# Prompt sparse attention rewritten block by block, key groups paired, probabilities scaled before their transposes

## The reference

```python
# 8 query heads, 2 key/value heads (K), 4 query heads for each (G), head dim 64
s = einsum('btkgd,bckd->bkgtc', qcg, k_cmp) * scale           # 63 compressed keys
p_cmp = _masked_probs(s, cmp_end <= q_pos)
o_cmp = einsum('bkgtc,bckd->btkgd', p_cmp, v_cmp)
imp = einsum('bkgtc,cs->bkts', p_cmp, c2s)                    # importance of 16 blocks of 64 keys
score = where(visible, imp + where(forced, 1e4, 0), NEG)
top_val, top_idx = top_k(score, 8)                            # 8 blocks chosen for each query and key head
p_sel = _masked_probs(q_rot @ k_sel, chosen and key_pos <= q_pos)
p_win = _masked_probs(q_rot @ kw, 0 <= q_pos - kw_pos < 512)  # sliding window
o = o_cmp * g[..., 0:1] + o_sel * g[..., 1:2] + o_win * g[..., 2:3]
```

## Time and profile before

| quantity | value |
|---|---|
| median of 3 runs | 3833.59 us |
| the profiled execution: its own time | 3827.84 us |
| its span in the trace | 3826.0 us |
| PE busy, of the span | 3136.7 us, 82% |
| DVE, ACT, POOL busy | 1184.1, 737.9, 273.9 us |
| mean granted clock of PE | 0.904 of full speed |

### The profile page before, as it was taken

How to read it: one execution, slowest core, us unless ns; L and a number is a source line. 1 busy time by engine, 2 the same in 40 slices (tenths; PEclk the granted TensorE clock), 3 DMA queues, 4 the chain that set the end, 5 groups by cost and what they waited for, 6 DMA issues and landing times. The chain is left out here.

```text
span 3826.0 us, 40607 instructions
## 1 busy us (share of the span) xinstructions
PE 3136.7 (82%) x13898; PEld 2038.5 (53%) x13898; DVE 1184.1 (31%) x2468; ACT 737.9 (19%) x1251; POOL 273.9 (7%) x291
## 2 busy tenths in 40 slices
PE   7886877775678999784566799667979999996999
PEld 4554546665556677552343344543446666664665
DVE  2333655453345555301230112221123323230000
ACT  3332431111023343200120111111111222120000
POOL 1110002221010101000000000000000010000000
PEclk9898988887589999897788899889989999998999
DMA  3111010001210000274755211352221111112211
GB/s 116 56 56 50 27 32 12 11 11 41 69 25 25 25 13 13 74 227 133 221 154 206 89 66 55 121 176 91 88 60 33 40 37 33 33 33 46 80 53 38
DMA packets 286044, 265.13 MB, mean 69 GB/s; under 512 B 68002, under 2 KB 250148, under 8 KB 285412
## 3 DMA queue, kind: packets, MB, share of 16 engines
q1 hardware_dynamic: 247684, 224.82, 18.8%
q10 hardware_dynamic: 38240, 38.84, 3.3%
HBM read 219.75 MB, written 48.04 MB: 70 GB/s over the span
## 5 line engine op out<-in xcount | busy, mean ns | idle before, releaser
L3030 PE MATMUL up_acc<-hnT,up_w 128*128 128x364 f32 (+1 forms) x2112 | 646.9, 470 | 11.6 <-DMA up_w<-in_w_up 11.6
L3030 PEld LDWEIGHTS up_acc<-hnT,up_w 128*128 128x128 f32 x2112 | 402.7, 191 | 255.5 <-issue 14.6
L3131 PE MATMUL down_acc<-mlp_gT,down_w 128*128 128x364 f32 (+1 forms) x1056 | 324.6, 471 | 29.9 <-DMA down_res<-scr_h2T 29.9
L3131 PEld LDWEIGHTS down_acc<-mlp_gT,down_w 128*128 128x128 f32 x1056 | 201.9, 191 | 152.6 <-issue 32.6
L391 PE MATMUL chan_acc<-xnT,chan_w 128*128 128x364 f32 (+1 forms) x576 | 185.6, 485 | 44.2 <-DMA chan_w<-in_w_in 28.1
L324 PE MATMUL proj_p<-proj_w_nat,proj_xT 128*128 128x512 f32 (+1 forms) x432 | 177.7, 575 | 14.2 <-ACT proj_xT L219 14.2
L391 PEld LDWEIGHTS chan_acc<-xnT,chan_w 128*128 128x128 f32 x576 | 112.7, 197 | 117.0 <-issue 53.9
L3069 DVE TENSOR_SCALAR up_y<-up_xp,up_tap 128x1024 f32<-128x1024 f32 x44 | 35.8, 812 | 425.0 <-ACT up_xs L3041 425.0
L324 PEld LDWEIGHTS proj_p<-proj_w_nat,proj_xT 128*128 128x128 f32 x432 | 88.2, 207 | 102.4 <-issue 79.7
L2590 PE MATMUL xo_p_h<-w_xo,xo_aT 128*128 128x512 f32 x288 | 128.0, 603 | 12.9 <-DVE xo_h L2545 10.7
L2612 PE MATMUL mixo_p_q<-w_xq,mixo_nT 128*128 128x512 f32 x288 | 127.6, 602 | 5.8 <-DVEq L2567 5.8
(11 more groups left out here) (538 smaller groups left out, 4443.5 us busy)
## 6 DMA issues: line engine op xcount, KB each, us to landing
up_w<-in_w_up SPq DMA_DIRECT2D x44, 512.0 KB, 4.5
sc_pg<-in_cache_cmp ACTq DMA_DIRECT2D x128, 128.0 KB, 2.8
sc_pg<-in_cache_cmp SPq DMA_DIRECT2D x128, 128.0 KB, 2.7
sa_ring<-in_cache_sel SPq DMA_DIRECT2D x128, 128.0 KB, 2.8
sa_ring<-in_cache_sel ACTq DMA_DIRECT2D x128, 128.0 KB, 2.8
down_w<-in_w_down SPq DMA_DIRECT2D x8, 1408.0 KB, 6.4
xs_kn<-in_cache_mem SPq DMA_DIRECT2D x8, 1024.0 KB, 6.7
xs_v<-in_cache_mem SPq DMA_DIRECT2D x8, 1024.0 KB, 9.5
```

The source lines that it names most:

```text
L3030: m = pe.matmul(acc[n][:, g, 0:b - a], w[:, s, n, k, :], hnT[:, k, a:b], start=(k == 0), stop=(k == KD - 1))
L3131: m = pe.matmul(acc[s][:, g, 0:b - a], w[:, s, f, :], gT[:, f, a:b], start=(f == 0), stop=(f == FT - 1))
```

## The change

The prompt's attention stage is written anew, with all loops unrolled:

- The unit of work is a "unit": one branch and one `g`, for the two key heads `kv` together (8 units a block, 64 in all). The queries of the two heads stand in rows 0 to 63 and 64 to 127 of one tile (`q_in`, `qT`). Each score product uses 64 rows of the array and writes to its own psum bank.
- The keys of a unit are exactly those that the block can see: b+1 tiles of 128 keys for the selected branch, min(b+1, 5) for the window. Over 512 keys a unit has two pieces. Blocks 0 to 3 have no mask from the top 8, since all of their key blocks are chosen. The importance sums, the top 8 and the mask are made for blocks 4 to 7 alone.
- The scores come out negated, so that the row minimum can serve as the bias of the exponential. DVE masks them and takes the minimum out of psum (L1660), ACT makes the exponentials in place (L1507).
- POOL computes gate / sum for the two heads of a unit and multiplies the probabilities by it, in place (`scale`, L1556 to L1564). The compressed probabilities are multiplied by their gate on DVE. Nothing is left to do at the end but to add the branches, which the psum accumulation does.
- A "round" (66 in all) handles one tile of 128 keys for all 8 heads: 8 transposes, a copy by ACT for the four heads of one key head (L1534) and one by DVE for the other (L1673), and two products with the values as weights (128 rows x 64 columns, one for each half of the array's columns) and 512 moving columns (L1429). The products of a round are issued after the transposes of the next round.
- The result is turned once for each block (L1495) and copied by ACT (L1538, L1544).
- `order()` lays down one order for all engines: in step i it interleaves the front of block i+2, the eight units of block i+1, the rounds of block i and the output of block i-1.
- In the stage before, keys and values of the window have no 512 leading zeros any more. The constants for the masks are one tile, `near`, instead of eight.
- In the cross-attention of the samples the sequence is now the innermost of the three loops.

```diff
-                sp.dma_start(vw[:, 4:, :], io["wrows"][0:SEQ, 128:256]...
+                sp.dma_start(vw[:, :, :], io["wrows"][0:SEQ, 128:256]...
...
-                act.activation(kw[:, WIN:WIN + 512], turned[2][:, :], ACT.Copy)
+                act.activation(kw[:, 0:512], turned[2][:, :], ACT.Copy)
...
-                dve.memset(kw[:, 0:WIN], 0.0)
-                dve.memset(vw[:, 0:4, :], 0.0)
...
+def rounds_of(b):
+    return [(WINB, k) for k in range(b + 1 - window_blocks(b), b + 1)] + [(SEL, k) for k in range(b + 1)]
+def unit(b, u):
+    branch, g = (WINB, u) if u < G else (SEL, u - G)
+    n = P * (window_blocks(b) if branch == WINB else b + 1)
+    return branch, g, P * (b + 1) - n, n, [(lo, min(512, n - lo)) for lo in range(0, n, 512)]
+FRONT = {0: "turn_q", 1: "cmp_scores", 2: "cmp_exp", 3: "cmp_norm", 4: "importance", 5: "top", 6: "turn_p", 7: "mask"}
+def order():
+    for i in range(-2, NQ + 1):
+        if i == NQ - 1:
+            yield "no_more_units", NQ, 0
+        if i == NQ:
+            yield "no_more_rounds", NQ, 0
+        for u in range(8):
+            if i >= 1 and u in (2, 3):
+                yield ("take_o", "turn_o")[u - 2], i - 1, 0
+            if i + 2 < NQ:
+                yield FRONT[u], i + 2, 0
+            if 0 <= i + 1 < NQ:
+                yield "unit", i + 1, u
+            if 0 <= i < NQ:
+                n = len(rounds_of(i))
+                for r in range(u * n // 8, (u + 1) * n // 8):
+                    yield "round", i, r
+ORDER = list(order())
...
+        def use(n):
+            b, branch, k = ROUNDS[n]
+            v = (vw if branch == WINB else vs)[:, k, :]
+            for kv in range(KVH):
+                pe.wait_ge(t_ready[kv], n + 1)
+            for kv in range(KVH):
+                pe.matmul(O[b % 2][HALF[kv], :], v[:, HALF[kv]], pT[:, n % 2, kv, :], start=False,
+                          stop=(n + 1 == FIRST_ROUND[b + 1]), skip_group_check=True).then_inc(pv_done[kv], 1)
...
+            elif what == "unit":
+                branch, g, at, _, parts = unit(b, x)
+                keys = kw if branch == WINB else ks
+                pe.wait_ge(*taken("turn_q", b))
+                for j, (lo, n) in enumerate(parts):
+                    out, read, before = slot(what, b, x, j)
+                    pe.wait_ge(read, before)
+                    for kv in range(KVH):
+                        pe.matmul(out[:, kv, 0:n], qT[HALF[kv], b % 2, 1, g * P:(g + 1) * P], keys[HALF[kv], at + lo:at + lo + n],
+                                  start=True, stop=True).then_inc(scored[kv], 1)
+            elif what == "round":
+                n = FIRST_ROUND[b] + x
+                branch, k = rounds_of(b)[x]
+                pe.wait_ge(scaled, 2 * (8 * b + (4 if branch == WINB else 8)))
+                c = (k - (b + 1 - window_blocks(b)) if branch == WINB else k) * P
+                for kv in range(KVH):
+                    pe.wait_ge(t_ready[kv], n)
+                    for g in range(G):
+                        t = pe.transpose(T[kv][:, g * P:(g + 1) * P], probs(b, branch, G * kv + g)[:, c:c + P], ident[:, :])
+                    t.then_inc(t_done[kv], 1)
+                if x == 0:
+                    pe.wait_ge(*taken("turn_p", b))
+                    if b >= 2:
+                        pe.wait_ge(oT_ready, b - 1)
+                    for kv in range(KVH):
+                        pe.matmul(O[b % 2][HALF[kv], :], vc[:, HALF[kv]], pcT[:, b % 2, kv, :], start=True, stop=False,
+                                  skip_group_check=True).then_inc(cv_done, 1)
+                if n:
+                    use(n - 1)
...
+        def exps(m):
+            b, u = m // 8, m % 8
+            branch, g, _, n, _ = unit(b, u)
+            act.wait_ge(low_ready, m + 1)
+            for kv in range(KVH):
+                p = probs(b, branch, G * kv + g)[:, 0:n]
+                act.activation(p, p, ACT.Exp, bias=low[:, b % 2, branch, g, kv:kv + 1], scale=-1.0,
+                               accum_out=sums[:, b % 2, branch, g, kv:kv + 1]).then_inc(exp_done, 1)
...
+        def scale(m):
+            b, u = m // 8, m % 8
+            branch, g, _, n, _ = unit(b, u)
+            c = coef[:, m % 2, :]
+            col = 3 * g + 1 + branch
+            pool.wait_ge(exp_done, KVH * (m + 1))
+            pool.tensor_scalar(c, sums[:, b % 2, branch, g, :], 1e-30, None, ALU.max)
+            pool.drain()
+            pool.tensor_tensor(c, c, minus_one[:, :], ALU.pow)
+            pool.drain()
+            pool.tensor_tensor(c, c, gates[:, b, col:col + 13:12], ALU.mult)
+            pool.drain()
+            for kv in range(KVH):
+                p = probs(b, branch, G * kv + g)[:, 0:n]
+                pool.tensor_scalar(p, p, c[:, kv:kv + 1], None, ALU.mult).then_inc(scaled, 1)
...
+            elif what == "unit":
+                branch, g, _, keys, parts = unit(b, x)
+                if branch == SEL and b >= 4:
+                    dve.wait_ge(mk_ready, b - 3)
+                for j, (lo, n) in enumerate(parts):
+                    out, read, _ = slot(what, b, x, j)
+                    for kv in range(KVH):
+                        if branch == SEL and b >= 4:
+                            mask = mk[:, b % 2, kv, lo:lo + n]
+                        else:
+                            mask = near[:, 640 - keys + lo:640 - keys + lo + n]
+                        low_to = low[:, b % 2, branch, g, kv:kv + 1] if len(parts) == 1 else piece_min[:, x % 2, j, kv:kv + 1]
+                        dve.wait_ge(scored[kv], piece_no[b, x, j])
+                        t = dve.tensor_tensor_reduce(probs(b, branch, G * kv + g)[:, lo:lo + n], out[:, kv, 0:n], mask, 1.0, -NEG,
+                                                     ALU.add, ALU.min, low_to)
+                    t.then_inc(read, 1)
+                dve.drain()
+                if len(parts) == 1:
+                    dve.sem_inc(low_ready, 1)
+                else:
+                    dve.tensor_tensor(low[:, b % 2, branch, g, :], piece_min[:, x % 2, 0, :], piece_min[:, x % 2, 1, :], ALU.min).then_inc(low_ready, 1)
+            elif what == "round":
+                n = FIRST_ROUND[b] + x
+                dve.wait_ge(t_done[1], n + 1)
+                if n >= 2:
+                    dve.wait_ge(pv_done[1], n - 1)
+                dve.tensor_copy(pT[:, n % 2, 1, :], T[1][:, :]).then_inc(t_ready[1], 1)
...
         m = pe.transpose(p_t[:, c * P:(c + 1) * P], p[:, c * P:(c + 1) * P], ident[:, :])
     m.then_inc(p_turned, 1)
     pe.wait_ge(p_ready, g + 1)
-    for b in range(4):
-        r = slice(32 * b, 32 * b + 32)
-        for n in range(2):
-            for c in range(2):
+    for n in range(2):
+        for c in range(2):
+            for b in range(4):
+                r = slice(32 * b, 32 * b + 32)
                 m = pe.matmul(p_o[r, n * 512:(n + 1) * 512], pT[:, c, r], v[:, 4 * g + b, c, n * 512:(n + 1) * 512], start=(c == 0), stop=(c == 1))
     m.then_inc(o_done, 1)
 
...
-    out["key_no"] = np.broadcast_to(np.arange(SEQ, dtype=f32), (P, SEQ))
-    out["q_no"] = np.arange(SEQ, dtype=f32).reshape(8, P).T
-    rr, cc, b = np.arange(P)[None, :, None], np.arange(640)[None, None, :], np.arange(8)[:, None, None]
-    out["win_bias"] = np.where((cc <= rr + 512) & (cc > rr) & (cc >= 512 - 128 * b), 0.0, NEG).astype(f32)
+    rr, cc = np.arange(P)[:, None], np.arange(640)[None, :]
+    out["near"] = np.where((cc <= rr + 512) & (cc > rr), 0.0, -NEG).astype(f32)
```

More of the change, by code:

```diff
@@ L1263, in _ @@
                 dve.wait_ge(turn_done, 8)
[L1264 removed]
+                dve.tensor_copy(kw[:, 512:SEQ], turned[3][:, :])
                 dve.drain()
@@ L1354, in run @@
-        def run(eng, pair):
-            with eng.Fori(0, 2) as i:
-                pair(i, False, False)
-            pair(2, True, False)
-            pair(3, True, True)
-        def heads(i, wide, last):
-            for p in range(2):
-                b = 2 * i + p
-                for h in range(8):
-                    nxt = None
-                    if h < 7:
-                        nxt = (b, p, h + 1, 8 * b + h + 1)
-                    elif not (last and p == 1):
-                        nxt = (b + 1, 1 - p, 0, 8 * b + 8)
-                    yield b, p, h, 8 * b + h, nxt, not (last and p == 1)
+        scaled = st.sem("scaled")
@@ new lines, in stage_nsa_prompt_attend @@
+        ORDER = list(order())
+        FIRST_ROUND = [sum(len(rounds_of(c)) for c in range(b)) for b in range(NQ + 1)]
+        ROUNDS = [(b, branch, k) for b in range(NQ) for branch, k in rounds_of(b)]
+        slot_uses, piece_no, pieces = {}, {}, 0
+        for what, b, u in ORDER:
+            if what in ("turn_q", "cmp_scores", "turn_p", "turn_o"):
+                slot_uses[what, b] = len(slot_uses)
+            elif what == "unit":
+                for j in range(len(unit(b, u)[4])):
+                    slot_uses[what, b, u, j] = len(slot_uses)
+                    piece_no[b, u, j] = pieces = pieces + 1
```

(34 more changed lines are left out.)

481 lines of the change are left out of this document (193 added, 288 removed).

## The result

| kernel | median of its runs, us | ratio to before, 95% interval |
|---|---|---|
| before | 3833.09 (4 runs, 3827.11 to 3834.82) | 1 |
| changed | 3675.5 (4 runs, 3670.3 to 3682.44) | 0.9593 [0.9573, 0.9612] |

The change gains 158 us, where I had forecast 222 and a time of 3611 us. The measured 3675.5 lies 7 us above the range's upper end, 3668. The sign was right and the size was not.

What follows compares the result with a forecast made beforehand. The attention stage was taken as PE bound; afterwards POOL leads small blocks, PE from block 3. Stage 21 + 257 + 28 + 8 + 10 = 324 against 540; 3827.8 - 216 - 7 = 3605, as median 3611 us, range 3575 to 3668.

Steps and rivals of the forecast that it cites:

- The step that failed: POOL's scaling of probabilities in the attention stage: 1.02 ns a column, 69 us, plus 128 x 0.12 = 15 us.
- order of the engines: Busiest engine in each step of the attention stage: POOL in the small blocks, PE from block 3 on; maxima sum to 224 us.
- Rival 1: POOL sets the attention stage's pace, scaling at the two-input price, 2.1 ns a column: stage 347, kernel 3634 us; chance 0.20.
- Start to the first units: Serial start of the attention stage: the first units come 21 us after the barrier.
- factor for hand-overs: Engines waiting for each other in the interleaved steps: 1.15 on 224 us, giving 257; bounds 1.05 and 1.35.
- Tail: End of the attention stage: 28 us of block 7's rounds alone, then 8 us for turning, storing and barrier.
- The samples' loop: Samples' cross-attention with column groups running side by side: 3.7 to 10.5 us gained, 7 taken.
- POOL's small instructions: Each unit's two small instructions, a power on 128x2 (0.71 us) and drains: 1.4 us, times 64 = 90 us.
- Rival 2: Score products on the two row halves don't run side by side: scores cost 56 us more, stage 368, kernel 3655; chance 0.14.
- The change of shape: PE switching tiling mode in the attention stage: 0.17 us each, 236 times, 40 us.
- Rival 3: Hand-overs between engines cost more than walked: factor 1.35, 302 us instead of 257, kernel 3656; chance 0.11.
- Rival 4: Slower than before, PE's rounds waiting for POOL's in-place scaling: stage 540 us at 5.3 ns a column, 3877 at 6; chance 0.02.

Runs made afterwards that it cites:

- kernel at the forecast price: Changed kernel, but POOL scales only 0.408 n - 68 of n columns (at least 8), so each scaling lasts about as predicted: 3586.44 us, ratio 0.9351.
- kernel with two passes: Changed kernel, but POOL passes over each tile a second time, multiplying by 1.0: 3886.68 us, ratio 1.0147.

## Why the prediction was off, step by step

**The step that failed** is POOL's: "The scaling itself, one wide input and one number a row, isn't in the trace ... I take 1.02, the row with one input: 69 us, plus 128 x 0.12 = 15." The scaling costs 67,584 x 2.50 ns = 169 us and 128 x 0.29 = 37: 206 where I had 84. With it went the order of the engines: I had PE as the busiest from block 3 on, and it was POOL nearly throughout. The kernel at the forecast price shows what the step is worth, 89 us of the whole. The copy in the earlier trace rows has one wide input too, but it does no arithmetic. POOL's two-input rows, 1.86 and 2.28 ns a column, were nearer, and even they were too low. The rule of the Trainium skill that I quoted (GPSIMD Engine Reference, Engine selection) compares POOL with DVE. Its half on two inputs, about twice as slow, fits here: 512 columns take 1.26 us on POOL by itself and 0.69 on DVE in the stage (L1633). Its half on one input, roughly line rate, fits the copy (1.01 ns a column) but not the multiplication: 1024 columns times a number take 2.84 us on POOL and 0.75 on DVE, each by itself. A bound by the nearest rows is no bound where no row has the operation.

**Rival 1 was the mechanism,** at 2.1 ns and with 3634. With the measured busy time of POOL its formula gives 304 x 1.05 + 21 + 36 = 376 for the stage, 381 with the 5 us that it had for the clock, and 395 was measured. The formula puts all of POOL's work before the last score product, and that isn't so: the product ends at 1399.1, and POOL scales until 1429.84, while PE cannot begin the last block's selected rounds. So the end takes 56 us instead of 36. Read along POOL's own list, the stage is the sum of three parts: 24.9 us to its first unit (1084.71), 345.1 to the end of its last scaling, and 25.0 behind it. POOL is busy for 303 of the 345 and waits 1.8 for another engine; the rest are the gaps between its instructions, which no run takes out. The prediction had 197 for this list, gaps counted in: the scaling makes 122 of the difference, the small instructions 12.

**The other terms,** read where POOL doesn't decide, in the kernel at the forecast price. Start to the first units 22 us (forecast 21). Steps 248, to set against 257 and 10 for the clock: the factor for hand-overs was 1.11 with the clock in it, not 1.15 and the clock on top. Tail 38 (36). Together 309 (by the profile's start and end) against 324. PE is busy for 262 us at a clock of 0.91 (forecast 242 at full clock). DVE took 188 in the changed kernel (forecast 216) and ACT 162 (166). The samples' loop gave 10, forecast 7 with 10.5 as its upper end. These errors, 25 us in all, made the time look nearer to the forecast than POOL's error alone would have left it; that is luck.

**POOL's small instructions:** 1.4 us a unit were forecast and 1.6 measured (1384.21 to 1385.80); the power on 128x2 takes 751 ns, forecast 710.

**Rival 2 is excluded:** eight passes of 512 columns on the two row halves take from 1386.78 to 1388.70, 1.92 us, 1.75 and the change of shape's 0.17, where one after the other would take 3.4. The change of shape costs the 0.17 us of the earlier trace rows again; the rule of the Trainium skill that I quoted for it (TensorEngine Tiling (Array Packing), Key Properties) names the drain, and the size comes from the rows. A round takes 2.03 us, forecast 2.05.

**Rival 3** has a factor of 1.35, and the kernel at the forecast price shows 1.11. **Rival 4** put the stage at 540 us when a column costs 5.3 ns. The kernel with two passes has 5.0 ns and took 608: POOL is busy for 500 us (rival 4 had 483), and the time beside it is 108 us where I had 57, about half of it gaps between POOL's instructions. So the crossing exists, at a price lower than I had put it.

**What was weighed wrongly** is the chance, too. The forecast's own range and rival 1 stood at 0.52 and 0.20 on a term that no row showed, on an engine that the sum itself had in front in three of the eight steps and within 20% of the front in four more. The range went by 2.1 ns. Even with the measured POOL time rival 1's formula gives 3663 to 3668, just inside; the late end of the stage took the time out.

## What to carry to other kernels

Before work is put on an engine that was idle, find a row of exactly that operation with those operands there; where there is none, let the range reach past the dearest row of that engine, since each us over its share counts in full once it leads (0.9 to 1.1 us here). When one engine trails, its waits turn up under the names of others, so look for the engine that never waits, not for the largest wait. On POOL, try a multiplication by one number a row as a product with a repeated operand (64 us here), give part of it to ACT (24 us more), and look at what DVE's instructions take beside it.

## What the runs showed of the hardware that I had not expected

- POOL, f32: multiplying 1024 columns by a number takes 2.84 us, by a repeated operand of a second input 1.89, by a second tile 2.34, copying 1.04. A constant is no cheaper (2.77).
- DVE's multiplication of 640 columns took 655 ns beside POOL's first form and 906 beside its second, with the longest at 2.26 us, and its minimum of two numbers a row 236 ns beside the first and 539 beside the second; ACT's (817 ns, against 821 for its exponentials of that width in the changed kernel) did not change.
- PE's granted clock in the stage was 0.81 when POOL led, 0.71 when POOL passed twice and 0.92 when it had little to do. PE's busy time for the same products was 279, 297 and 259 us.
